# S5 maps by three real products, and the RG-LRU recurrence with roots in pairs, gate products in front and scan steps moved

## The reference, cut to what matters

```python
def s5_scan(u, a_re, a_im, log_dt, b_re, b_im, c_re, c_im):   # 64 groups, 64 states, 16 channels
    ...
    bb_re = co_re[..., None] * b_re - co_im[..., None] * b_im
    bb_im = co_re[..., None] * b_im + co_im[..., None] * b_re
    ...                                  # s[t] = a * s[t-1] + bb * u[t], complex
    y = einsum(sr, c_re) - einsum(si, c_im)

def rglru_scan(xc, wa, ba, wx, bx, lam):                      # 4 heads of 256 channels
    r = sigmoid(xh @ wa + ba)
    ig = sigmoid(xh @ wx + bx)
    log_a = -RG_C * r * softplus(-lam)
    a = exp(log_a)
    bterm = sqrt(-expm1(2.0 * log_a)) * (ig * xf)
    h[t] = a[t] * h[t-1] + bterm[t]      # forward, and backward with other weights
```

## Time and profile before

| | |
|---|---|
| median of three runs | 2925.86 us (2925.67 to 2931.95) |
| profiled execution | 2930.73 us |
| its span | 2929.2 us |
| its mean granted TensorE clock | 0.959 of full speed |
| PE / PE weight loads busy | 2712.4 / 2077.0 us |
| DVE, ACT, POOL busy | 1542.7, 819.7, 1020.8 us |

### The profile page before, as it was taken

One profiled execution on the slowest core, in us unless ns is written; L12 is line 12 of the kernel. 1 busy time (PEld: TensorE's weight loads), 2 busy tenths in 40 slices (PEclk: granted clock), 3 DMA queues, 4 the chain that ended last, 5 costly groups with the idle time before them and its releaser, 6 DMA issues.

```text
span 2929.2 us, 37626 instructions
## 1 busy us (share of the span) xinstructions
PE 2712.4 (93%) x13237; PEld 2077.0 (71%) x13237; DVE 1542.7 (53%) x2348; ACT 819.7 (28%) x989; POOL 1020.8 (35%) x1177
## 2 busy tenths in 40 slices
PE   7997779989998999989997999989899999999998
PEld 2457655444445777878886777768898988888787
DVE  3439755878775222441326555596546455555611
ACT  2315542561642112220213111211314232331310
POOL 0019977877700001011123333345433334342000
PEclk9999889999999998999998999999999999999999
DMA  7213221101105667351114222346313131214521
GB/s 289 78 58 98 86 82 29 47 29 47 40 21 171 189 192 253 82 194 41 33 33 106 93 100 100 133 146 229 121 64 102 34 108 64 103 40 137 165 85 45
DMA packets 257688, 297.98 MB, mean 102 GB/s; under 512 B 34928, under 2 KB 217496, under 8 KB 257184
## 3 DMA queue, kind: packets, MB, share of 16 engines
q1 hardware_dynamic: 201568, 206.60, 22.2%
q10 hardware_dynamic: 51168, 73.04, 6.9%
q0 software_dynamic: 4832, 16.78, 2.0%
HBM read 203.09 MB, written 93.29 MB: 101 GB/s over the span
## 4 chain that ended last, share of the span: by engine, by line
PE 66%; DVE 11%; ACT 3%; issue 3%; DMA 1%; POOL 1%; DVEq 0%; ACTq 0%; SPq 0%; POOLq 0%
PE ps L132 57%; PE ps L1219 5%; PE ps L1060 1%; PE ps L1066 1%; DVE s_scan_tmp L2011 1%; DVE arena L2013 1%; DVE s_scan_tmp L2009 1%; DVE xc_part L2305 1%; DVE arena L491 1%; DVE arena L2062 0%; ACT arena L1392 0%; ACT L1392 0%; DVE arena L2031 0%; PE ps L1224 0%; DVE arena L2055 0%
## 5 line engine op out<-in xcount | busy, mean ns | idle before, releaser
L132 PE MATMUL ps<-arena,weights 128*128 128x512 f32 (+2 forms) x2432 | 751.6, 487 | 52.9 <-ACT arena L1392 19.8
L132 PEld LDWEIGHTS ps<-arena,weights 128*128 128x128 f32 (+1 forms) x2432 | 397.7, 177 | 397.0 <-issue 323.0
L132 PE MATMUL ps<-h_part,in_weight_parts 128*128 128x512 f32 (+1 forms) x1920 | 414.5, 377 | 14.9 <-DVE arena L2223 9.4
L132 PEld LDWEIGHTS ps<-h_part,in_weight_parts 128*128 128x128 f32 x1920 | 339.9, 191 | 85.6 <-issue 17.2
L132 PE MATMUL ps<-v_part,p_part 128*128 128x512 f32 x1248 | 296.7, 397 | 0.1
L132 PEld LDWEIGHTS ps<-v_part,p_part 128*128 128x128 f32 x1248 | 235.4, 191 | 49.7 <-issue 0.9
L132 PE MATMUL ps<-q_part,xc_part 128*128 128x256 f32 x1920 | 248.5, 289 | 14.7 <-DVE v_part L2305 10.8
L132 PEld LDWEIGHTS ps<-q_part,xc_part 128*128 128x128 f32 x1920 | 238.1, 195 | 16.3 <-DVE v_part L2305 11.5
L1219 PE MATMUL ps<-wo_part,mx_part 128*128 128x512 f32 x768 | 184.0, 400 | 5.7 <-DVE mx_part L2305 4.7
L2632 POOL TENSOR_TENSOR in_weight_parts<-weights,ones 128x1024 fp32r<-128x1024 f32 x32 | 79.0, 2468 | 303.4 <-PE ps L132 186.7
L1219 PEld LDWEIGHTS ps<-wo_part,mx_part 128*128 128x128 f32 x768 | 145.3, 191 | 40.6 <-issue 4.9
(11 more groups left out here) (372 smaller groups left out, 4095.0 us busy)
## 6 DMA issues: line engine op xcount, KB each, us to landing
weights<-in_e_w_in SPq DMA_DIRECT2D x32, 512.0 KB, 4.1
weights<-in_o_w_in SPq DMA_DIRECT2D x32, 512.0 KB, 4.1
s_out_maps<-arena ACTq DMA_DIRECT2D x16, 640.0 KB, 3.0
weights<-in_mod_w POOLq DMA_DIRECT2D x20, 512.0 KB, 4.8
arena<-s_out_maps SPq DMA_DIRECT2D x16, 640.0 KB, 4.3
ml_xcv<-arena ACTq DMA_DIRECT2D x16, 640.0 KB, 3.0
xc_full<-ml_xcv SPq DMA_DIRECT2D x4, 2560.0 KB, 9.1
xm_tiles<-ml_xm SPq DMA_DIRECT2D x16, 640.0 KB, 3.8
```

What stands on the lines that cost most here:

```text
L132: return nc.tensor.matmul(o, lhsT, rhs, start=(k == 0), stop=(k == n - 1))
```

## The change

Products: with `BBsum` = re + im of `BB`, `PWEsum` likewise, and the difference stored in place of the imaginary part of `PWE`, DVE makes three products per block; one of them (powers' real part times `BBsum`) serves both the real and the imaginary part in PE's transposes. POOL likewise makes three products and two differences. DVE prepares the sums once. The number of matmuls is the same. `nident`, `vtmp` and the buffers move to other addresses.

RG-LRU: ACT takes `root(0)` and `root(1)` together after unit 1, `root(2)` and `root(3)` after unit 3; the sigmoids of units 2 and 3 wait for the product of the recurrence that frees their buffer (`rg_mul`) and for its scan (`rg_dir`). DVE does `gated` of both tiles of a direction and then both recurrences. Scan steps: before, 10, 8, 4 (ahead of the first silu product), 4 (ahead of the second), then 3, 3, 4, 4 in `gated`; after, 10, 8, 1 + 1 (ahead of the first silu product), 1 (ahead of the second), 7 behind it, then 4, 0, 4, 4.

```diff
@@ PE, transposes @@
-                            mm(ps[:, r, P * g:P * g + P], X[:, s, r, g], ident[:, :], 0, 2)
+                            mm(ps[:, r, P * g:P * g + P], X[:, s, g], ident[:, :], 0, 2)
                             last = mm(ps[:, r, P * g:P * g + P], Xw[s][r][:, P * g:P * g + P], (nident, ident)[r][:, :], 1, 2)
@@ ACT, RG-LRU @@
-                    if u >= 2:
-                        act.wait_ge(*past("rg_dir", 4 * i + (u - 1)))
-                    for m, (dst, c0) in enumerate(((RT, C_BA), (IT, C_BX))):
+                    for m, (dst, c0, free) in enumerate(((RT, C_BA, "rg_mul"), (IT, C_BX, "rg_dir"))):
+                        if u >= 2:
+                            act.wait_ge(*past(free, 4 * i + (u - 1)))
                         act.wait_ge(*past(f"rg_gmm{m}", 4 * i + (u + 1)))
...
-                    if u:
-                        root(u - 1)
...
-                root(3)
+                    if s == 1:
+                        root(u - 1)
+                        root(u)
@@ DVE, tables @@
+            V.tensor_tensor(BBsum, BB[:, 0], BB[:, 1], ALU.add)
+            V.tensor_tensor(CTsum, CT[:, 0], CT[:, 1], ALU.add)
+            V.tensor_tensor(PWFsum, PWF[:, :, 0], PWF[:, :, 1], ALU.add)
+            link(V.tensor_tensor(PWEsum, PWE[:, :, 0], PWE[:, :, 1], ALU.add))
+            V.tensor_tensor(CT[:, 1], CT[:, 0], CT[:, 1], ALU.subtract)
+            V.tensor_tensor(PWE[:, :, 1], PWE[:, :, 1], PWE[:, :, 0], ALU.subtract)
@@ DVE, state_maps @@
-                V.tensor_tensor(xo(x[0]), pw(0), bb(0), ALU.mult)
-                V.tensor_tensor(xo(Xw[s][0]), pw(1), bb(1), ALU.mult)
-                V.tensor_tensor(xo(x[1]), pw(0), bb(1), ALU.mult)
-                V.tensor_tensor(xo(Xw[s][1]), pw(1), bb(0), ALU.mult).then_inc(sem(f"x_ready{s}"), 1)
+                V.tensor_tensor(xo(X[:, s].rearrange("p g c -> p (g c)")), pw(PWE[:, :, 0]), bb(BBsum), ALU.mult)
+                V.tensor_tensor(xo(Xw[s][0]), pw(PWEsum), bb(BB[:, 1]), ALU.mult)
+                V.tensor_tensor(xo(Xw[s][1]), pw(PWE[:, :, 1]), bb(BB[:, 0]), ALU.mult).then_inc(sem(f"x_ready{s}"), 1)
@@ DVE, RG-LRU @@
-                scan_steps(4)
+                scan_steps(1)
                 for s in range(2):
-                    scan_steps(4 * s)
+                    scan_steps(1)
                     dve.wait_ge(*past("rg_sg", 2 * i + s + 1))
                     V.tensor_tensor(SG[:, s], ps3[s], SG[:, s], ALU.mult).then_inc(sem(f"rg_ev{s}"), 1)
+                scan_steps(7)
...
-                    scan_steps((3, 3, 4, 4)[u])
+                    scan_steps((4, 0, 4, 4)[u])
...
-                    ilink(V.tensor_tensor(IT[:, s], IT[:, s], RT[:, s], ALU.mult))
+                    V.tensor_tensor(IT[:, s], IT[:, s], RT[:, s], ALU.mult).then_inc(sem("rg_mul"), 1)
+                    dve.wait_ge(*past("rg_mul", 4 * i + (u + 1)))
...
-                for u in range(4):
-                    gated(u)
-                    recurrence(u)
+                for d in range(2):
+                    for s in range(2):
+                        gated(2 * d + s)
+                    for s in range(2):
+                        recurrence(2 * d + s)
@@ POOL, output maps @@
-                    GP.tensor_tensor(Gv[s][:, :, 0], pw(0), cc(0), ALU.mult)
-                    GP.tensor_tensor(go(pg1), pw(1), cc(1), ALU.mult)
-                    GP.tensor_tensor(Gv[s][:, :, 1], pw(1), cc(0), ALU.mult)
-                    GP.tensor_tensor(go(pg2), pw(0), cc(1), ALU.mult).then_inc(sem("pool_g"), 1)
+                    GP.tensor_tensor(go(pg1), pw(PWFsum), cc(CT[:, 0]), ALU.mult)
+                    GP.tensor_tensor(Gv[s][:, :, 0], pw(PWF[:, :, 1]), cc(CT[:, 1]), ALU.mult)
+                    GP.tensor_tensor(Gv[s][:, :, 1], pw(PWF[:, :, 0]), cc(CTsum), ALU.mult).then_inc(sem("pool_g"), 1)
...
-                    GP.tensor_tensor(Gv[s][:, :, 0], Gv[s][:, :, 0], go(pg1), ALU.add)
-                    GP.tensor_tensor(Gv[s][:, :, 1], Gv[s][:, :, 1], go(pg2), ALU.subtract).then_inc(sem(f"g_ready{s}"), 1)
+                    GP.tensor_tensor(Gv[s][:, :, 0], go(pg1), Gv[s][:, :, 0], ALU.subtract)
+                    GP.tensor_tensor(Gv[s][:, :, 1], go(pg1), Gv[s][:, :, 1], ALU.subtract).then_inc(sem(f"g_ready{s}"), 1)
```

More of the change, by code:

```diff
@@ L83 @@
     ("x_ready0", NB // 2), ("x_ready1", NB // 2), ("v_mm0", NB // 2), ("v_mm1", NB // 2))
-MID_SIGNALS = {"diag_ready": ("diag0", 1), "scale_row": ("scale0", 1), "sq_total": ("sq_sum", DT - 1), "sq_added": ("mod_row", 5), "ss_mm1": ("mod_cols", 1),
+MID_SIGNALS = {"rg_mul": ("diag0", 1), "diag_ready": ("rg_mul", 4 * RH), "scale_row": ("scale0", 1), "sq_total": ("sq_sum", DT - 1), "sq_added": ("mod_row", 5), "ss_mm1": ("mod_cols", 1),
     "xcv_stored0": ("mod0_in2", 16), "z_stored0": ("mod0_in3", 16), "z_stored1": ("mod0_in4", 16),
@@ L234, in build @@
         cn = rb(2048, 2048).rearrange("p (h r q) -> p h r q", r=2, h=HC)
-        X = rb(0, 2048).rearrange("p (s r g c) -> p s r g c", s=2, r=2, g=GB)
+        X = rb(0, 1024).rearrange("p (s g c) -> p s g c", s=2, g=GB)
+        BBsum = rb(1024, 1024).rearrange("p (h g) -> p h g", h=HC)
+        CTsum = rb(10240, 1024).rearrange("p (h g) -> p h g", h=HC)
+        PWEsum = rb(13824, 512).rearrange("p (k g) -> p k g", g=G)
+        PWFsum = rb(5504, 640).rearrange("p (k g) -> p k g", g=G)
         Gb = [rb(2048, 1280), rb(14336, 1280)]
@@ L238, in build @@
         BT = rb(4096, 2048).rearrange("p (r h g) -> p r h g", r=2, h=HC)
-        t1 = rb(4096, 1280)
         CT = rb(6144, 2048).rearrange("p (r h g) -> p r h g", r=2, h=HC)
@@ L285, in build @@
         tB = at(YTo + 2560, 2048).rearrange("p (r h g) -> p r h g", r=2, h=HC)
[L286 to L289, removed]
+        pg1 = rb(3840, 640)
+        nident = rb(11264, P)
+        Xw = [[rb(4480, 512), GW[:, 1536:2048]], [rb(4992, 512), rb(3328, 512)]]
         AO = rb(0, DT * TOK).rearrange("p (k t) -> p k t", k=DT)
@@ L304, in build @@
         m_d = bass.AP(v_d.tensor, 0, [[HC * LAG * HC, G], [LAG * HC, HC], [HC, T], [1, P]])
-        vtmp = GW[0:HC, 1536:1536 + GB * HC].rearrange("p (g h) -> p g h", g=GB)
+        vtmp = rb(11392, GB * HC)[0:HC].rearrange("p (g h) -> p g h", g=GB)
         GWv = GW[:, :].rearrange("p (d m k n) -> p d m k n", d=2, m=2, k=2)
@@ L1937, in state_maps, with pw, bb @@
                 gs = bass.ds(GB * b, GB)
[L1939 to L1943, removed]
+                def pw(x):
+                    return x[:, :, gs].rearrange("p k g -> p g k").unsqueeze(2).to_broadcast([P, GB, HC, T])
+                def bb(x):
+                    return x[:, :, gs].rearrange("p h g -> p g h").unsqueeze(3).to_broadcast([P, GB, HC, T])
                 def xo(ap):
@@ L1948, in state_maps @@
                 dve.wait_ge(*past(f"x_t{s}", i))
-                x = [X[:, s, r].rearrange("p g c -> p (g c)") for r in range(2)]
-                V.tensor_tensor(xo(x[0]), pw(0), bb(0), ALU.mult)
-                V.tensor_tensor(xo(Xw[s][0]), pw(1), bb(1), ALU.mult)
-                V.tensor_tensor(xo(x[1]), pw(0), bb(1), ALU.mult)
-                V.tensor_tensor(xo(Xw[s][1]), pw(1), bb(0), ALU.mult).then_inc(sem(f"x_ready{s}"), 1)
+                V.tensor_tensor(xo(X[:, s].rearrange("p g c -> p (g c)")), pw(PWE[:, :, 0]), bb(BBsum), ALU.mult)
+                V.tensor_tensor(xo(Xw[s][0]), pw(PWEsum), bb(BB[:, 1]), ALU.mult)
+                V.tensor_tensor(xo(Xw[s][1]), pw(PWE[:, :, 1]), bb(BB[:, 0]), ALU.mult).then_inc(sem(f"x_ready{s}"), 1)
             def lag_matrices(i, s, n):
@@ L1992, in _ @@
             s1, s2 = SPs[1]
-            n0, per = link_n[0], 19
+            n0, per = link_n[0], 15
             with dve.Fori(0, RH) as i:
@@ L2530, in _, with pw, cc @@
                     gs = bass.ds(GB * (2 * i + s), GB)
[L2532 to L2536, removed]
+                    def pw(x):
+                        return x[:, :, gs].rearrange("p k g -> p g k").unsqueeze(3).to_broadcast([P, GB, SL, HC])
+                    def cc(x):
+                        return x[:, :, gs].rearrange("p h g -> p g h").unsqueeze(2).to_broadcast([P, GB, SL, HC])
                     def go(ap):
```

1 line of the change is left out of this document (removed).

## The result

The changed kernel took 2899.41 us in the median of four runs (2895.76 to 2902.33), the kernel before 2926.65 beside it (2925.67 to 2931.95): a ratio of 0.9903, 95% interval 0.9885 to 0.9920. That is 27 us faster where 38 were forecast, inside the range of 2879 to 2901, near its slow end. The profiled execution has a span of 2900.8 against 2929.2, so 28.4 less.

What follows compares the result with a forecast made beforehand. POOL was taken to bound the S5 maps; DVE delayed RG-LRU's gates, PE set its third round. Maps 31.2 (36.7 less 5.5) plus RG-LRU 7.0 (8.8 - 0.2 - 1.6) made 38.2: median 2925.86 to 2887.7 us, range 2879 to 2901.

Steps and rivals of the forecast that it cites:

- The likeliest case: Whole kernel: POOL's saving in the maps plus the RG-LRU gain, 2882 to 2893 us, chance 0.61.
- rival 3: RG-LRU: the rearrangement gives nothing, DVE's lateness passing through root 1 to the next projections; 2895 us, chance 0.12.
- the slow 1.7: RG-LRU, unit 3: 24 PE records taken at 10.56 us after an idle, against 8.86 in a like place.
- Maps, POOL: S5 maps: one product less per block on POOL and on DVE shortens POOL's work by 36.7 us.
- Six operations in front: Ahead of the S5 maps: six new DVE operations delay POOL's start, unhidden, by 5.5 us.
- rival 2: S5 maps: PE takes over as the bound at a granted clock of 0.74, losing 16 us; 2904, chance 0.13.
- rival 4: S5 maps: PE stays at 1.2 GHz through whole blocks, making the kernel slower; 2982 us, chance 0.02.
- Moved steps: RG-LRU: fewer scan steps before the silu products shorten two rounds from 117.3 to 112.9 us, 8.8 together.
- Roots in pairs give nothing there: RG-LRU: next projections start 32.8 us after T0 (ACT starting unit 0's second sigmoid), against 32.6 before.
- Third round: RG-LRU: PE sets this round, which loses 0.2 us, giving 110.9.
- Tail: RG-LRU, from the last round's start to the stretch's end: 1.6 us lost, giving 61.7.
- the lock of the port pair: S5 maps: each DVE product would block POOL for its full 1.10 us; 7.6 more gain, 2880.1, chance 0.12.

Runs made afterwards that it cites:

- s5_only: The S5 maps part of the change alone, with single roots and scan steps as before, against the kernel before: 2894.12 us, ratio 0.9875.
- steps_single: The changed kernel, but with single roots in the old order; maps and moved scan steps kept: 2888.73 us, ratio 0.9852 to the kernel before.
- run 7: The changed kernel plus a one-column sigmoid on ACT ahead of the wait for the recurrence's product: 2891.52 us, ratio 0.9870 to the kernel before.
- rg_only: The RG-LRU part of the change alone, S5 maps as before, against the kernel before: 2928.47 us, ratio 0.9992.
- pairs_primed: Same kernel as run 7: the change plus a one-column sigmoid that loads ACT's table before the wait: 2891.52 us.
- runs 5 and 6: Against s5_only, one engine back to four products per block: DVE in the first (2908.0 us), POOL in the second (2921.57 us).
- pairs_oldsteps: The changed kernel, but with scan steps ahead of the silu products as before: 2907.39 us, ratio 0.9921 to the kernel before.

## Why the prediction was right, and where it was not

The direction and the range held. The likeliest case, 2882 to 2893, did not: what came true is nearest to rival 3, the rearrangement of the RG-LRU that gives nothing (2895 forecast, 2899.4 measured). It did not come by rival 3's route, a DVE late for root 1 (root 1 ended on time), but by PE's lower clock after an idle, which the sum held as "the slow 1.7" and priced too low. That the total stayed inside the range is in part luck: the maps gave 2.5 us more than forecast in the profile (5.7 in the median of s5_only), and the RG-LRU part 9.8 less.

- **Maps, POOL** (forecast 36.7 less): POOL's span is 38.1 shorter. 48 DVE products at (163.35 - 134.1) / 48 = 0.61 each, in place of 0.64, are the difference. Right.
- **Six operations in front** (5.5): 5.47. Right. One of 1024 elements takes 1.23, of 640 0.82 and of 512 0.68; by their elements the short ones would be 0.76 and 0.61. The sum of the six is 5.86, and 0.4 of it goes by overlap at their ends. Together the maps were forecast at 31.2 and gave 33.7 in the profile, 36.9 alone in the median.
- **PE's clock in the maps** (rival 2), **1.2 GHz throughout** (rival 4): PE waits for POOL 19.1 us in eleven blocks, and POOL's heads idle 2.8 + 2.2 as before. So POOL stayed the bound, and both fall.
- **Moved steps** (8.8 in two rounds): alone 11.2 in the stretch. Right in kind and somewhat low. With single roots PE doesn't wait for the silu products at all any more: in steps_single the projections and the gate groups behind them are one piece.
- **"Roots in pairs give nothing there"** (next projections at T0 + 32.8): this is the step that failed. Point by point in the first round: root 1 ends at 19.4 (forecast 19.5), fine. Unit 2's first sigmoid starts at 21.4, not 20.8: the table load waits with it (run 7). PE idles 4.63, not 4.1. And "I take 10.56" for unit 3 was 11.2 to 11.8 in all four rounds; unit 3 ends at 33.9. Everything on ACT and DVE behind it is late by the same, DVE's last product ends at 62.6 (forecast 61.6), the convolution at 100.9 (99.6). Then the second miss: the gate groups, forecast at 9.1 for their part in front of T0, start after an idle of 2.10 to 2.95 and the first 24 records take 10.57, at a granted clock of 0.84. Those two terms make 115.5 of 112.9. The trace of before had this price in it. The 4.58 that the prediction took for both gate groups is the second one's; the first started 6.41 ahead of it, and its 12 records took 6.20 at a granted clock of 0.72:

```profile
725.77 19.57 PE L132 MATMUL ps<-arena,weights 128*128 128x512 f32 x48 [4.58 <-DVE arena L2038]
```

- **Third round** (110.9): 111.4. **Tail** (61.7): 63.4, of which unit 3's 11.81 in place of 10.56 is 1.25.
- The whole stretch: 2.6 + 3.7 + 0.5 for the rounds, 1.7 for the tail and 1.2 ahead of the first T0 (80.44 where it was 79.22) are 9.7 more than forecast, so that a gain of 7.0 became a loss of 2.8. The 1.2 isn't the pairs' doing: the part ahead of the first T0 is 80.0 in s5_only, with single roots, and 79.1 in rg_only, with pairs and the old maps.

The sentence "without the slow 1.7 it would be 9.7" was the sound part: with PE kept at work the stretch is 484.54 - 473.54 = 11.0 shorter than before. The sum had the clock as a detail of one group, with one price for it, and as nothing for the gate groups behind the next wait. It was the largest term.

The switch of tables can be read in the trace of pairs_primed: load at 490.31, just after the roots, and the next operation at 491.61, so 1.30 per switch. The Trainium skill (ScalarE: Activation LUTs, "What ACT_TABLE_LOAD costs") puts a drain on top, 2.66 in all; no drain shows here. The other rule that the prediction weighed is the lock of the port pair. In runs 5 and 6 a DVE product of 1.10 costs POOL 0.64. By the Trainium skill (SBUF — State Buffer, "SBUF: two separate sides") the loser is blocked for the whole instruction; the trace agrees only in part, since both engines do slow one another down, but not by the whole 1.10.

Left open: why the work ahead of the changed part starts up to 2.6 us apart from run to run (POOL's first operation at 211.96 and 214.56 with equal code in front), why the slow time after an idle falls where it does, and whether pairs or single roots are better once both have the clock. By the stretches single roots are (470.2 against 473.5 and 474.0), by the medians nothing can be said.

## What to carry to other kernels

When PE idles for a few microseconds in front of a dense group, look up in the trace what such groups took after every wait, and price this one and those behind the next waits by the whole spread, the slowest included; here the clock cost more than the wait itself. Taking table loads away from ACT helps where ACT is what others wait for: here two loads fewer per round bought a wait in the chain to PE. And try the halves of a change apart, since a good half (the moved steps) can hide a bad one (the pairs).

## What the runs showed of the hardware that I had not expected

- Matmuls with an unused result made a kernel faster by 13.8 us in a stretch of 487, with the granted clock at 1.00 through the groups behind two waits. With single roots, where PE idled 2.8 and not 4.6, two and two of them made the stretch 3.0 shorter, which the median doesn't show.
- The same 24 records took 8.86 at a granted clock of 1.00 and up to 11.90 (0.74) behind an idle of 2 to 5 us, and the length of the idle doesn't settle which. After 2.81 they took 8.86, 10.24 to 10.56 or 11.90, in rounds that were otherwise alike; after 4.6 they took from 10.25 (rg_only) to 11.89 (pairs_oldsteps), and never 8.86. The 11.90 is in PE's timeline of steps_single:

```profile
828.07 11.90 PE L132 MATMUL ps<-arena,weights 128*128 128x512 f32 x24 [2.81 <-ACT arena L1393]
```

- The load of the activation table in front of an operation also stood behind the wait in front of that operation (idle 0.68, then the load of 1.28), and didn't use the waiting time; a one-column operation of the same table ahead of the wait (0.20 us) does.
- A DVE product that takes 1.10 alone costs POOL 0.61 to 0.64 when they run together, and then takes 1.9 to 2.4 itself.
